# Two of the six weight parts of an expert issued from ScalarE's queue instead of SyncE's

## The reference, cut to what matters

```python
gates = jax.nn.softmax(top_val, axis=-1)          # top 4 of 32 router logits
...
gu = xblk @ w_gate_up[e] + b_gate_up[e]           # 1024 x 2048 weights, f32
x_glu, x_lin = jnp.split(gu, 2, axis=-1)
x_glu = jnp.minimum(x_glu, SWIGLU_LIMIT)
x_lin = jnp.clip(x_lin, -SWIGLU_LIMIT, SWIGLU_LIMIT)
act = x_glu * jax.nn.sigmoid(SWIGLU_ALPHA * x_glu) * (x_lin + 1.0)
return act @ w_down[e] + b_down[e]                # 1024 x 1024 weights, f32
```

## Time and profile before

| | |
|---|---|
| median of 3 runs | 1269.91 us (1266.95 to 1271.45) |
| profiled execution, own time | 1272.87 us |
| its span in the profile | 1271.0 us |
| TensorE, VectorE, ScalarE busy | 93%, 36%, 19% of the span |
| DMA queue q1 (SyncE's) | 428.64 MB, 80.3% of the 16 engines' span |
| DMA queue q10 (ScalarE's) | 1.45 MB, 0.4% |
| TensorE waits for gate-up weights (L1897) | 48.0 us, 43 times |

### The profile page before, as it was taken

One profiled execution on the slowest core, in us unless ns is written; L12 is line 12 of the kernel. 1 busy time (PEld: TensorE's weight loads), 2 busy tenths in 40 slices (PEclk: granted clock), 3 DMA queues, 4 the chain that ended last, 5 costly groups with the idle time before them and its releaser, 6 DMA issues. The chain is left out here.

```text
span 1271.0 us, 16440 instructions
## 1 busy us (share of the span) xinstructions
PE 1179.7 (93%) x6522; PEld 558.6 (44%) x6522; DVE 459.4 (36%) x899; ACT 242.5 (19%) x426; POOL 80.1 (6%) x81
## 2 busy tenths in 40 slices
PE   7999999998999999999898999899999999998987
PEld 4666699657343442433333333434343333333332
DVE  5989645216442313132222231332232313222225
ACT  2244455223210101111010101021010111101012
POOL 1100143533000000000000000000000000000000
PEclk9899999997899999999999999999999999999997
DMA  9411210048899999999999999799999999999993
GB/s 376 191 67 67 89 26 2 13 166 318 356 427 428 428 429 429 429 429 428 428 429 428 427 427 428 306 402 427 429 429 428 428 429 427 428 429 427 427 426 143
DMA packets 35080, 433.74 MB, mean 341 GB/s; under 512 B 4736, under 2 KB 5120, under 8 KB 9216
## 3 DMA queue, kind: packets, MB, share of 16 engines
q1 hardware_dynamic: 32624, 428.64, 80.3%
q0 software_dynamic: 800, 3.08, 0.7%
q10 hardware_dynamic: 1616, 1.45, 0.4%
HBM read 428.50 MB, written 4.65 MB: 341 GB/s over the span
## 5 line engine op out<-in xcount | busy, mean ns | idle before, releaser
L1897 PE MATMUL bank<-ring,win 128*64 128x512 f32 x1984 | 442.3, 595 | 48.9 <-DMA ring<-in_w_gate_up 48.0
L1897 PEld LDWEIGHTS bank<-ring,win 128*64 128x64 f32 x1984 | 138.1, 137 | 335.4 <-issue 231.4
L1920 PE MATMUL bank<-ring,win 128*64 128x512 f32 x992 | 221.5, 599 | 0.3 <-issue 0.3
L1360 DVE TENSOR_SCALAR win<-bank 128x512 f32<-128x512 f32 x33 | 22.8, 691 | 402.8 <-PE bank L1897 380.9
L1920 PEld LDWEIGHTS bank<-ring,win 128*64 128x64 f32 x992 | 70.1, 138 | 133.4 <-issue 129.4
L845 ACT ACTIVATE win<-win 128x512 f32<-128x512 f32 x33 | 20.8, 630 | 447.9 <-DVE win L1360 447.9
L853 ACT ACTIVATE win<-bank 64x512 f32<-64x512 f32 x64 | 37.9, 592 | 279.0 <-PE bank L1920 264.9
L1294 DVE TENSOR_TENSOR win<-win,qkvc 128x1024 f32<-128x1024 f32 x16 | 19.6, 1225 | 143.0 <-ACT qkvc L871 143.0
L1354 DVE TENSOR_TENSOR xt<-xt,bank 128x512 f32<-128x512 f32 x108 | 67.9, 679 | 5.1 <-PE bank L1870 4.7
L1876 PE MATMUL bank<-qkvc,win 128*128 128x512 bf16 x288 | 67.7, 380 | 1.9 <-DVE xt L1354 1.9
L986 DVE SCALAR_TENSOR_TENSOR cb<-ring,par,cb 128x384 f32<-128x384 f32 x120 | 66.5, 609 | 0.8
(11 more groups left out here) (312 smaller groups left out, 1094.8 us busy)
## 6 DMA issues: line engine op xcount, KB each, us to landing
ring<-in_w_gate_up SPq DMA_DIRECT2D x127, 2048.0 KB, 24.4
ring<-in_w_down SPq DMA_DIRECT2D x63, 2048.0 KB, 21.9
win<-in_w_in SPq DMA_DIRECT2D x3, 2048.0 KB, 10.1
ring<-in_w_in SPq DMA_DIRECT2D x2, 2048.0 KB, 13.2
win<-in_w_out SPq DMA_DIRECT2D x2, 2048.0 KB, 8.3
ring<-in_w_gate_up SPq DMA_DIRECT2D x2, 1024.0 KB, 11.0
out_ss<-ring POOLq DMA_DIRECT2D x1, 2048.0 KB, 9.3
ring<-in_w_down SPq DMA_DIRECT2D x2, 1024.0 KB, 22.1
```

Of the source, the lines that this page charges most:

```text
L1360: dve.tensor_scalar(g_s, bank[low], LIMIT, None, ALU.min).then_inc(g, 1)
L1897: mm = pe.matmul(bank[half][a * BLK:(a + 1) * BLK], xs[:, k], ring[:, c:c + 512], start=False, stop=(k == KD - 1), skip_group_check=True)
L1920: mm = pe.matmul(bank[7][a * BLK:(a + 1) * BLK], actT[:, q * P + j * BLK:][:, 0:BLK], ring[:, c:c + 512], start=(k == 0), stop=(k == KD - ...
```

## The change

`load_piece`, which issues one part's DMA, moves to where ScalarE's program can call it too. In the loop over experts 2 to 28 SyncE leaves out parts 3 and 5 (`BY_SCALAR`). ScalarE reads the expert's number itself (`number_of`), and issues part 3 of the next expert behind the sigmoid of this one, and part 5 behind the copies of this one's down result. In the wide unit part 5 stands behind all four copies. Experts 0, 1 and 29 to 31 stay with SyncE in full.

```diff
+BY_SCALAR = (GU - 1, NPART - 1)
...
             with sp.Fori(2, NE - 3) as e:
                 number = sp.value_load(expert_no[0:1, bass.ds(e, 1)], min_val=0, max_val=NE - 1)
-                load_expert(sp, number, lambda s: e * USES + (USED[s] - USES))
+                for r in range(NPART):
+                    if r not in BY_SCALAR:
+                        sp.wait_ge(s_wu, e * USES + (USED[r] - USES))
+                        load_piece(sp, number, r, 0, GQ if r < GU else DQ)
...
-            def pair(u, turn, first=False):
+            def load_behind(number, turn, r):
+
+                act.wait_ge(s_wu, turn * USES + USED[r])
+                load_piece(act, number, r, 0, GQ if r < GU else DQ)
+
+            def number_of(turn):
+                return act.value_load(expert_no[0:1, bass.ds(turn, 1)], min_val=0, max_val=NE - 1)
+
+            def pair(u, turn, first=False, loads=(False, False)):
 
                 if not first:
                     y_split(u - 1)
+                if loads[0]:
+                    number = number_of(turn + 1)
                 sigmoid(2 * u)
+                if loads[0]:
+                    load_behind(number, turn, GU - 1)
                 rows_out(0, 7, turn, None if first else u)
+                if loads[0]:
+                    load_behind(number, turn, NPART - 1)
                 hits_t(u)
+                if loads[1]:
+                    act.wait_ge(s_tabs, 1)
+                    number = number_of(turn + 2)
                 sigmoid(2 * u + 1)
+                if loads[1]:
+                    load_behind(number, turn + 1, GU - 1)
                 rows_high(u + 1)
                 rows_out(1, 7, turn + 1)
+                if loads[1]:
+                    load_behind(number, turn + 1, NPART - 1)
 
             def wide_unit():
 
                 y_split(MID - 1)
+                number = number_of(WIDE + 1)
                 sigmoid(2 * MID)
+                load_behind(number, WIDE, GU - 1)
                 sigmoid(2 * MID + 1)
                 rows_high(MID + 1)
                 hits_t(MID)
                 rows_out(0, 7, WIDE, MID)
                 rows_out(1, WIDE_BANK, WIDE)
+                load_behind(number, WIDE, NPART - 1)
```

More of the change, by code:

```diff
@@ L408, in stream_step, with load_piece @@
         block = ctx.enter_context(nc.Block())
+        def load_piece(ld, e, r, q0, q1, done=None):
+            if r < GU:
+                rows_of, width, src = GQ, 2 * F, w_gate_up[bass.ds(e, 1), r * GQ * P:(r + 1) * GQ * P, :]
+            else:
+                rows_of, width = DQ, D
+                src = w_down[bass.ds(e, 1), (r - GU) * DQ * P:(r - GU + 1) * DQ * P, :]
+            src = src.rearrange("a (p q) n -> (a p) (q n)", q=rows_of)
+            ld.dma_start(ring[:, PART_AT[r] + q0 * width:PART_AT[r] + q1 * width], src[:, q0 * width:q1 * width])\
+              .then_inc(done or s_w[r], 16)
         @block.sync
@@ L456, in _ @@
             sp.wait_ge(s_dec, NB)
[L458 to L467, removed]
             def load_expert(ld, e, value):
@@ L894, in wide_unit @@
                 rows_out(1, WIDE_BANK, WIDE)
+                load_behind(number, WIDE, NPART - 1)
             rows_high(0)
             h_split()
-            pair(0, 0, first=True)
+            pair(0, 0, first=True, loads=(False, True))
             with act.Fori(1, MID) as u:
-                pair(u, 2 * u)
+                pair(u, 2 * u, loads=(True, True))
             wide_unit()
-            with act.Fori(MID + 1, NU - 2) as u:
-                pair(u, 2 * u - 1)
+            with act.Fori(MID + 1, NU - 3) as u:
+                pair(u, 2 * u - 1, loads=(True, True))
+            pair(NU - 3, 2 * (NU - 3) - 1, loads=(True, False))
             act.wait_ge(s_tabs, 2)
```

## The result

| | before | changed |
|---|---|---|
| median of 11 runs each | 1271.24 us (1266.95 to 1274.28) | 1277.72 us (1274.38 to 1282.1) |
| profiled execution, own time; span | 1272.87; 1271.0 us | 1280.12; 1278.1 us |

The ratio is 1.0048, with a 95% interval from 1.0034 to 1.0063: the changed kernel is 6.1 us slower (4.3 to 8.0). The profiled pair lies 7.1 us apart in its spans.

A forecast was written before the change was run, and what follows sets the result against it. The bound was one gapless DMA line at 428 GB/s, with a hole at the wide unit. Lateness of 5.7 to 8.4 us, plus 2.4, plus a little clock, taken as 10.0, gave 1280 us; range 1269 to 1290.

The forecast's parts named there:

- The line, not latency: Weight DMAs: parts queue in one gapless line at 428 GB/s; the 25.5 us to landing is queueing, not latency.
- Work added on ScalarE, SyncE's shorter list: 0: Experts 2 to 28: ScalarE's added DMAs and number loads hide in its idle time, and SyncE gains nothing: 0.
- Equal halves: Two full queues on the 16 engines: each is assumed to get half the bandwidth, so ScalarE's parts overtake.
- Lateness into the wide unit: At expert 16: TensorE arrives 5.7 to 8.4 us late because overtaking parts are moved early, lengthening the DMA hole.
- the 8.4 us case: Entering the wide unit: TensorE is 8.4 us late if expert 15 is the one with the long wait.
- rival B: Through the experts: slower still, from clock falls or too small a share for ScalarE's queue; 1292 us, chance 0.12 over +15 us.
- The sign that the prediction set for B: TensorE's clock below 0.97 in 440 to 780 us would show the slower-still rival.
- Part 5 issued behind four copies: Wide unit: part 5's DMA waits behind four copies in ScalarE's list while the line is empty, +2.4 us.
- The tail, 0: After the wide unit: the line does not run dry and parts from expert 29 come in order, so 0.
- The written signs: Profile: 113 MB on q10, 428 GB/s, waits of 5 to 6 us, wide unit 6 to 8 us later, hole 18 to 20.
- Rival A: Both queues: parts land about as asked, order costs nothing, only 2.4 us in the wide unit remain; 1272 us, chance 0.15.
- rival C: Saturated stretches: two queues feed the engines better, rate up over 1.3%; 1265 us at 2%, chance 0.13.

The follow-up runs named there:

- x_second: Changed kernel, but ScalarE issues parts 3 and 5 of experts 18 to 28 only; 1270.4 us, ratio 0.9994 to before.
- x_pause: Changed kernel, but experts 11 to 17 are SyncE's again, ScalarE keeping 2 to 10 and 18 to 28; 1270.91 us, ratio 0.9994 to before.
- x_part3: Changed kernel, but ScalarE issues only part 3, part 5 staying with SyncE; 1272.5 us, ratio 1.0020 to before.
- x_first: Changed kernel, but ScalarE issues parts 3 and 5 of experts 2 to 17 only; 1278.39 us, ratio 1.0066 to before.
- x_wide_late: Changed kernel plus a wait: in the wide unit ScalarE issues part 5 only after its four copies finish; 1284.04 us, ratio 1.0094 to before.

## Why the prediction was right

The range (1269 to 1290 us), the sign and the mechanism held; the forecast of 1280 us was 2.3 us above the median of 1277.72. Against the median of before in the same runs the change cost 6.5 us where I had summed 10. That the sum came this near is in part luck: it held 2.4 us for part 5 that are not there, and lacked about as much for the clock at the wide unit.

**The line, not latency.** Right, up to the last experts. Every kernel with a rate of 428 GB/s and the old hole has the old time, whatever its waits look like (x_second, x_pause).

**Work added on ScalarE, SyncE's shorter list: 0.** Right, by the same two.

**Equal halves.** Right, and this was the choice with the least behind it. It is 54.5% and 45.0% in one window shown, 49.6% and 52.2% in the other. The rule of the Trainium skill, DMA: Bandwidth & Descriptors, "Queues, rings and completion order", says that each DMA engine takes turns between the queues that have work, packet by packet; the halves agree with it, and no run here shows the single turns. ScalarE's parts land after 14 us and not 11. The working had 9.8 us for a part beside another, and the moving takes about that. It had nothing for the time between issue and first bytes, some 3 us in the x_part3 window, and between the last bytes and the landing. A part that has the line for itself does not land after 4.90 us either; the one issued at 820.81 us by the kernel before took 7.6 (issues of 820 to 821 us):

```profile
ring<-in_w_down SPq DMA_DIRECT2D x1, 2048.0 KB, 7.6
```

**Lateness into the wide unit, forecast 5.7 to 8.4 us.** Right in mechanism, too small in size: 8.5 to 10.6 us. The working put the long wait before part 2 of every second expert. The trace has it in every second or third; the last one before the wide unit falls on expert 15 in all three profiles of the changed kernel, which is the 8.4 us case. What was missing is the clock. The low stretch begins about when that wait ends, and parts 2 and 3 take 9.73, 8.67 and 9.70 us in the three profiles, 8.44 in x_first and 8.59 in x_wide_late, where 7.09 is the full clock's time. That is 2.6 us where the low stretch lasts 6.8 us (+10.6 and +10.3 on the ruler) and 1.35 to 1.6 us where it lasts 3.4 (+8.6, +8.5, +8.5). Without it the lateness is 7.0 to 8.0 us, inside the forecast. I had let the slack of two experts pay for the clock; just before the wide unit there is no expert left to pay. The prediction named that exception and gave it half a microsecond.

**The fall of the clock, rival B's mechanism.** It happens, as the page on the clock gate says of waits for a DMA (the Trainium skill, TensorE: Matmul & The Clock Gate, "HAM oscillation"), but once per long wait and not twice in two experts. The sign that the prediction set for B, a clock below 0.97 in 440 to 780 us, came true in two of the three profiles of the changed kernel: 0.96, 0.97 and 0.96. It was a bad sign, as it counts falls and not what they cost: x_pause has 0.98 there and x_second 0.97 behind the wide unit, both at the old time, so rival B as a cost in every expert is out. With waits of up to 1.6 us (x_part3) the clock did not fall in the experts; with 3.5 us and more it did; of those from 2.38 to 3.02 us some had a fall behind them and some had none.

**Part 5 issued behind four copies, +2.4 us.** Wrong. This is the step that failed. The sum took the place of the DMA in ScalarE's list for its time. ScalarE's sequencer issues the DMA while the copies before it are still being worked on, 0.15 us behind the start of the first: the only semaphore that it waits for is `s_wu`. Counted from part 4's issue, part 5 leaves ScalarE after 836.97 - 830.06 = 6.91 us, and it left SyncE after 7.26 - 0.33 = 6.93. The step is worth 0.0 us. x_wide_late shows what it would have looked like.

**The tail, 0.** Not quite, with two errors that go opposite ways. The line does not run dry, as forecast, but TensorE can be the later one at the end: 3.2 us in one of three profiles. And the last combining with what follows it took 16.4 us before and 14.3 after, by the clock, 2.1 us in the changed kernel's favour. That the latter is the change's doing is not shown.

**The sum again, from the three profiles of either kernel, as means:** start-up -0.8, lateness 9.8, part 5's place 0.0, from there to the last gate-up matmul +1.2, end -2.1: 8.1 us, which is the difference of the mean spans, beside 6.1 (4.3 to 8.0) from the timed runs. Start-up varies by 3 us within the changed kernel alone and the end by 2.6, so their differences are not shown to be the change's.

**The written signs.** Met: q10 carries 114.70 MB (113 and the 1.45 that it had), the rate is 428 GB/s. Missed in size: the hole is 17.6 us (18 to 20 were forecast), the long wait up to 4.9 us in 500 to 780 us (5 to 6), ScalarE's parts land after 14 us (11), and the wide unit comes later than the 6 to 8 us forecast.

Rival A (order without effect) is out by the ruler, and rival C (a higher rate) by the 428 GB/s.

## What to carry to other kernels

When one queue is served without a gap and in the order of need, moving some of its transfers to a second queue adds no bandwidth; it gives the moved ones a share of their own, and with a third of the bytes and half of the engines they arrive early at the cost of those needed sooner. That doesn't show as time until the consumer has to be on time for something: look for the place where the line runs dry, and for the end of the kernel, and ask how late the consumer comes there. A change can also look harmless in half of the program (x_second) and be paid in the other half.

The place of a DMA in an engine's list is not its time: ask what it waits for, not what stands ahead of it.

## What the runs showed that I had not expected

- ScalarE issues a DMA 0.15 us behind the start of the first of four copies that stand before it, 2.3 us before the last ends.
- A fall of the clock in a wait costs only what it still covers behind the wait: 2.6 us and 1.35 to 1.6 us here.
- A long wait three experts before the end leaves TensorE behind the line at the end: 3.2 us in one of three profiles.
- The last combining takes 5.4 or 8.0 us by where the clock falls in it: 8 us in all three profiles of the kernel before; in nine profiles of the others 5.4 us seven times and 8 us twice.
